# Another order of the rows within each expert's 64-row tile, in a two-layer MLA, sliding-window and MoE step

## The reference

```
def hier_moe(x, ...):                      # 32 experts in 4 groups of 8, FF = 512
    g_p, g_idx = top_k(softmax(xt @ w_group + b_group), 1)
    e_top, e_idx = top_k((xt @ w_expert + b_expert) of that group, 2)
    gate = g_p * softmax(e_top)
    ...
    hid = silu(xb @ w_gate[e]) * (xb @ w_up[e])     # xb: the rows of expert e
    yb = hid @ w_down[e]
    y = sum over a token's two experts of gate * its row of yb
```

## Time and profile before

| | us |
|---|---|
| median of three runs | 1774.24 |
| the runs | 1773.89, 1774.24, 1779.27 |
| the profiled execution | 1780.06 |
| its span, first to last instruction | 1778.4 |
| PE busy | 1677.9 |
| DVE busy | 651.8 |
| ACT busy | 381.2 |
| POOL busy | 216.2 |

### The profile page before, as it was taken

The page is one execution under the profiler, slowest core; times in us unless marked ns, Lnnn a source line. Parts: engine busy times, 40 slices in busy tenths (PEclk is TensorE's granted clock), DMA queues, the critical chain, the costliest instruction groups (busy, mean ns, idle before and its releaser), DMA issues.

```text
span 1778.4 us, 27879 instructions
## 1 busy us (share of the span) xinstructions
PE 1677.9 (94%) x9782; PEld 822.3 (46%) x9783; DVE 651.8 (37%) x1593; ACT 381.2 (21%) x878; POOL 216.2 (12%) x313
## 2 busy tenths in 40 slices
PE   7899899889899999999998899999899999999995
PEld 5466665545544444444443445455344444444432
DVE  2333588742322222222221656764322222222214
ACT  2233445531111111111110234342111111111112
POOL 1232025400010000101011201000001010101000
PEclk9899999989999999999999899999899999999997
DMA  6154139875489999999998800135799999999994
GB/s 188 50 157 115 28 124 309 282 273 224 157 343 404 422 416 423 410 422 413 421 411 335 306 1 1 28 136 227 274 386 418 420 420 419 417 414 417 410 378 159
DMA packets 84883, 513.81 MB, mean 289 GB/s; under 512 B 20821, under 2 KB 43302, under 8 KB 58586
## 3 DMA queue, kind: packets, MB, share of 16 engines
q1 hardware_dynamic: 66378, 463.45, 64.8%
q0 software_dynamic: 18416, 49.16, 8.5%
HBM read 499.65 MB, written 26.52 MB: 296 GB/s over the span
## 4 chain that ended last, share of the span: by engine, by line
PE 80%; DMA 7%; DVE 6%; issue 2%; ACT 2%; DVEq 1%; SPq 1%; ACTq 1%; POOLq 0%
PE ps L2080 72%; PE ps L2085 8%; DMA mem<-in_moe_w_up 4%; DMA mem<-in_cache_mla 2%; ACT mem L801 1%; DVE mem L1373 1%; SPq L482 1%; DVE mem L1859 0%; ACTq L982 0%; DMA mem<-in_mla_w_a 0%; DMA mem<-moe_rows_back 0%; DVE mem L1830 0%; DVEq L1381 0%; DVE mem L1822 0%; DMA mem<-in_mla_wq_b 0%
## 5 line engine op out<-in xcount | busy, mean ns | idle before, releaser
L2080 PE MATMUL ps<-mem 128*64 128x512 f32 (+14 forms) x8398 | 1513.9, 477 | 55.3 <-ACT mem L801 14.8
L2080 PEld LDWEIGHTS ps<-mem 128*64 128x64 f32 (+5 forms) x8398 | 659.0, 146 | 825.3 <-issue 741.4
L801 ACT ACTIVATE mem<-ps 128x512 f32<-128x512 f32 (+7 forms) x358 | 193.5, 546 | 552.6 <-PE ps L2080 392.0
L2085 PE MATMUL ps<-mem 64*128 64x64 f32 (+3 forms) x1384 | 202.6, 281 | 37.7 <-issue 7.6
L2085 PEld LDWEIGHTS ps<-mem 64*128 64x128 f32 (+3 forms) x1384 | 168.3, 182 | 122.2 <-issue 97.4
L1698 DVE TENSOR_TENSOR mem<-mem,ps 64x512 f32<-64x512 f32 x64 | 44.1, 690 | 408.0 <-ACT mem L1051 407.8
L736 POOL DMA_INDIRECT moe_rows_back<-mem x64 | 57.3, 896 | 818.6 <-DVE mem L1716 810.3
L1051 ACT ACTIVATE mem<-ps 64x512 f32<-64x512 f32 x64 | 37.7, 589 | 519.2 <-PE ps L2080 519.2
L1373 DVE STREAM_TRANSPOSE mem<-mem 128x2560 f32<-128x2560 f32 x32 | 89.2, 2824 | 17.5 <-DMA mem<-in_cache_mla 17.2
L1716 DVE COPY mem<-ps 64x512 f32<-64x512 f32 x64 | 44.4, 693 | 133.3 <-PE ps L2080 133.2
L686 POOL DMA_DIRECT2D mem<-in_cache_mla x96 | 51.5, 537 | 75.5 <-PE ps L2080 68.2
(11 more groups left out here) (238 smaller groups left out, 534.2 us busy)
## 6 DMA issues: line engine op xcount, KB each, us to landing
mem<-in_moe_w_gate SPq DMA_DIRECT2D x64, 2048.0 KB
mem<-in_moe_w_up SPq DMA_DIRECT2D x64, 2048.0 KB
mem<-in_moe_w_down SPq DMA_DIRECT2D x64, 2048.0 KB
mem<-in_cache_mla POOLq DMA_DIRECT2D x160, 160.0 KB, 3.6
mem<-in_cache_mla SPq DMA_DIRECT2D x96, 160.0 KB, 4.5
mem<-moe_rows_back SPq DMA_DIRECT2D x8, 1024.0 KB, 8.9
mem<-in_mla_wkv_b SPq DMA_DIRECT2D x8, 512.0 KB, 6.5
mem<-in_mla_wo SPq DMA_DIRECT2D x1, 4096.0 KB, 14.2
```

Source lines behind the costliest of these rows:

```text
L801: return act.activation(out, in_, ACT.Copy)
L2080: return pe.matmul(out, lhsT, rhs, start=start, stop=stop)
L2085: return pe.transpose(out, in_, ident[at:at + n, at:at + n])
```

## The change

A table `spread` with two rows of 64 numbers is added and filled once by DVE. `spread[0]` holds, at row c * 32 + 2 * e + a of the tile, the rank c * 32 + 16 * a + e (c and a are 0 or 1, e is 0 to 15); `spread[1]` the same with 15 - e for e. `mark` compares with `spread[b]`, where b is 0 for even experts and 1 for odd ones, instead of `slots`; the loop over extra blocks compares with `spread[0]`. So of an expert with n rows, the first 16 stand one in each pair of rows of the tile's lower half, the next 16 fill these pairs, and the rest do the same in the upper half; in odd experts the pairs are taken from the other end. The tensor `mem` grows by 80 words and `keep` by 128, so that what lies behind moves.

```diff
-        WORDS = 53120
+        WORDS = 53200
...
         consts = mem[:, TILES * D:keep.at]
+        spread = [keep.take(BLK) for _ in range(2)]
...
             latent_T(PT)
+            by_rank = slots.rearrange("p (c a e) -> p c a e", c=2, a=2)
+            by_row = [s.rearrange("p (c e a) -> p c a e", c=2, a=2) for s in spread]
+            v.tensor_copy(by_row[0], by_rank)
+            for e in range(BLK // 4):
+                v.tensor_copy(by_row[1][:, :, :, BLK // 4 - 1 - e:BLK // 4 - e], by_rank[:, :, :, e:e + 1])
             v.tensor_copy(pick.rearrange("p j (i r) -> p j i r", i=4),
...
                 def mark(q, b):
 
                     v.tensor_tensor(onehot[b], rankm[:, :, cols(q, 1)].broadcast_to([P, TILES, BLK]),
-                                    slots.unsqueeze(1).broadcast_to([P, TILES, BLK]), ALU.is_equal
+                                    spread[b].unsqueeze(1).broadcast_to([P, TILES, BLK]), ALU.is_equal
                                     ).then_inc(sig["onehot_ready"], 1)
...
                         v.tensor_tensor(onehot[0], shift.unsqueeze(2).broadcast_to([P, TILES, BLK]),
-                                        slots.unsqueeze(1).broadcast_to([P, TILES, BLK]), ALU.is_equal
+                                        spread[0].unsqueeze(1).broadcast_to([P, TILES, BLK]), ALU.is_equal
                                         ).then_inc(sig["more_marks"], 1)
```

## The result

The changed kernel takes 1767.05 us (median of 19 runs, 1761.32 to 1775.18). The kernel before, run beside it and before it, takes 1778.57 us (median of 19, 1772.46 to 1783.2). The ratio on record is 0.995 with a 95% interval of 0.9939 to 0.9961, that is 6.9 to 10.8 us less; the two medians by themselves are 11.5 us apart. A later repeat gave 0.995 again (0.9931 to 0.9969). The profiled execution went from 1780.06 to 1769.54 us.

What follows compares the result with a forecast made beforehand. PE sets the pace until each MoE stage's last experts, where weights come late behind one or two overloaded DMA engines. 7.0 (layer 0) + 6.5 (layer 1) = 13.5 us off gives 1762.0 us, own range 1757 to 1767, wide 1757 to 1771.

Steps and rivals of the forecast that it cites:

- The map and the rows: Both MoE stages: DMA engine j serves rows 2j, 2j+1, 32+2j, 33+2j; busiest falls from 149 to 112 and 156 to 116.
- blocks of four: Rival map for the MoE tiles: engine j serves rows 4j to 4j+3, so no change, 1772 us; chance 8%.
- handicap: Slower rival: engine 15 slow of itself, hidden under its few rows; at 8 us 1778, at most 1789; chance 4%.
- the costs put at nothing: DVE's 17 new copies, at most 3.9 us, covered by its idle time; other table and shifted addresses: zero.
- The slow clock: PE's slower clock behind late weights at the stages' ends: 1.70 us in layer 0, 2.80 in layer 1, to go.
- I take 5.2, the smaller: Layer 0's end: busiest DMA engine finishes 5.2 us earlier, the estimate from tails, not 5.9 from its rows; layer 1 5.3.
- layer 1's 6.5 us: Layer 1's end: both PE waits for weights and the slow clock go, 0.48 + 3.25 + 2.80 us.
- all engines late together: Rival: evened queues still behind PE, waits of 0.2 to 1 us stay; gain 9 to 10, 1765 to 1769; chance 12%.
- a margin of 0.8 us: Layer 0's end: last weights there at 942.6, PE asks for them at 943.35, so waits of 4.5 us go.
- so I take 966.5: Joint between the layers: layer 0's last scatter lands at 966.5, between 963.0 and 968.8, 7.0 us before 973.5.
- Layer 0 in all: Layer 0's end and the joint to layer 1: 7.0 us less, 4.5 of it the waits.
- The base: Whole kernel: profiled execution lay 5.8 us above the runs' median; 1762.0 leaned to 1760.7 rather than 1766.5.

Runs made afterwards that it cites:

- e4: Changed kernel with ranks 4j to 4j+3 all put on rows 2j, 2j+1, 32+2j, 33+2j in all experts: 1790.22 us, 1.0089 of the kernel before.
- e3: Changed kernel with even experts in rank order and odd ones in that order with pairs taken from 15 down: 1774.39 us, 0.9996 of the kernel before.
- e1: Changed kernel with both tables filled in rank order, keeping tables, copies and addresses: 1777.94 us, 1.0016 of the kernel before.
- e7: Changed kernel with ranks 4j to 4j+3 on one engine, odd experts from the other end: 1790.66 us, 1.0079 of the kernel before.
- e8: Changed kernel with only the even experts' ranks 4j to 4j+3 put on one engine: 1773.96 us, 0.999 of the kernel before.
- e6: Changed kernel with the second part of layer 1's wqkv issued behind SP's first load of rows_back: 1770.63 us, 0.9954 of the kernel before.
- e5: Changed kernel with the gathers' index bound at 0, so odd experts' gathers carry no rows: 1755.72 us, 0.9894 of the kernel before.
- e2: Changed kernel with ranks dealt over the pairs from pair 0 up in all experts, no reversal: 1767.94 us, 0.9967 of the kernel before.

## Why the prediction was right or wrong

**The map and the rows** were right. Rank order in the same code gives the old time, the increments of layer 1's last scatter show the rows where the map has them (2, 1 and 13 engines with none, one and two rows before, 9, 1 and 6 with none, three and four in e4), blocks of four are refuted by e4's 1.0089 too and rows j, j + 16 by e3, and the lag fell from 6.6 to 1.5 us in layer 0 and from 6.8 to 1.4 in layer 1: by 5.1 and 5.4 us, where 5.2 and 5.3 had been forecast. By the map engine 15 has nearly the most rows after the change (111 of 112 and 116 of 116), and the lag of 1.5 and 1.4 us is no longer than the rows make it (1.5 and 1.8): no handicap shows here.

**Right: the costs put at nothing.** e1 bounds copies, other table and addresses together at -0.02% to +0.34%; DVE shows 4.95 us of idle behind the copies where I had said some 4.

**The slow clock.** The sums use 1.70 and 2.80 us for it. They are 12.22 and 13.32 us less 10.52 for the same 48 records, and what the runs show of its cause is the granted clock beside them: before, 0.60 in 932.93 to 937.00 and 0.50 in 1726.80 to 1729.00, behind waits of 1.60 and 3.25 us; after, 0.50 in 1717.66 to 1720.00, behind the wait of 1.34 us. Behind those of 1.16 us before and 0.54 after the block took 10.52 us.

**Wrong: the size of the step "I take 5.2, the smaller".** The last up weights came only 3.5 us earlier in layer 0 (from 947.81 to 945.91, though PE came to this stretch 1.63 us later) and 3.8 in layer 1 (from 1726.80 to 1717.66, of which 5.35 us are PE's own earlier arrival, 1667.38 to 1662.03). I had let the busiest engine fall to a mean that stands still. It does not stand still: the mean landing of the last down weights came 1.4 us later in layer 0 (49.9 to 51.3) and 1.5 in layer 1 (50.7 to 52.2), and 5.1 - 1.4 = 3.7 and 5.4 - 1.5 = 3.9 are near the 3.5 and 3.8 found.

Why the mean came later is less sure. The order of the odd experts' rows can move the rate, as e7 and e8 show (409 and 404 GB/s against 416 and 412), and in layer 0 the two kernels in rank order have the earliest means (49.9 and 50.2) and the highest rate (417) of those that gather rows; the others with a mean in the table have 50.8 to 52.1 and 415 or 416. But in layer 1 rank order in the new code has a mean of 51.8, 1.1 us later than the same order before: two executions can differ by most of the 1.5 us. Dealt one way has 50.2 there, the earliest. That the new order itself costs the rate something is likely in layer 0 and open in layer 1. Nor is it clear why the pairs reversed have so late a mean (53.6) in layer 1: their rates in the table, 415 and 412, are those of the repeated changed kernel, which keeps its gain.

So 0.54 and 1.34 us of wait stayed, one with a slow clock of 1.68 us behind it. Of layer 1's 6.5 us only 6.53 - 1.34 - 1.68 = 3.5 went; 1.70 more came from the slow stretch at 1680 that went too. I had put it at nothing because I had not seen it; it hung on the same late weights, and the sum would have been 1.70 us larger, and further off, with it. This is the rival "all engines late together", to which I gave 12%: its 9 to 10 us and 1765 to 1769 are what happened (10.5 us in the profile, 8.9 by the ratio, 1767.05). It is also the sign of being wrong that I had named, a tail that shrinks while waits stay. Its condition was there to be read: a margin of 0.8 us in layer 0 under a sum whose one term, 5.2, had no allowance for the rate. For layer 1 I had a margin of 1.5 us, and 1.34 us of wait stayed all the same.

**Wrong: the step "so I take 966.5".** Scatter landed at 971.2, and 968.1 was forecast (966.5 and the 1.63 us by which this execution was late). I reasoned that most engines are idle two to three microseconds after the issue. That was true of the uneven queue, where 14 of the 16 engines had landed their rows 4.81 us after the issue; in the even one most work until 968 to 970 (share 1.03 in 967 to 968, 0.55 in 969 to 970), the scatter's rows stand behind their loads, and the first engine lands its rows 5.89 us after the issue. The worst end that I gave, the new end of the busiest engine, was nearly the right one: 968.8 + 1.63 = 970.4. Layer 0 in all gave 4.6 us and not 7.0. e6 and e5 show the cause: with wqkv's bytes moved or the queues shorter the scatter takes 3.6 us.

**The base.** 1762.0 leaned on a median of 1774.24 us of three runs. Nineteen gave 1778.57. That is 4.3 us of the 5.05 by which the time was missed. The gain itself was forecast as 12.2 us from the median; it was 11.5 between the medians and 8.9 by the ratio. So the direction and the mechanism were right and the gain was forecast too large, by about 3 us in the profiled execution. 1767.05 lies inside the wide range (1757 to 1771) and just outside my own (1757 to 1767).

## What to carry to other kernels

When a transfer carries few rows, count bytes per DMA engine, not per transfer. Here the busiest engine had, by the map, 46 and 51 rows over the mean of 103 and 104.5, and the last down weights, split over all 16, landed 6.6 and 6.8 us behind the mean of their increments; with 9 and 12 rows over it was 1.5 and 1.4 us. Evening it out helped only down to the length of the queue as a whole: 0.54 and 1.34 us of wait stayed, which went when the gathers carried no rows. A small DMA that had slipped in behind idle engines then stood behind busy ones: the first increments of layer 0's last scatter came 2.45 us after its issue before and 5.89 us after. Before taking a queue's mean as fixed, compare its GB/s at full share with and without the odd transfers in it, here 416 and 413 against 427 and 425.

## What the runs showed of the hardware

- In a GpSimd-issued indirect DMA of 64 rows of 4096 B, one engine serves rows 2j, 2j+1, 32+2j and 33+2j, for j from 0 to 15 (that j is also the engine's number is my naming; the traces name no engine). This rests on the increments of layer 1's last scatter (13 engines with two of 27 rows in rank order at 2.33 to 2.54 us, 6 with four in e4 at 2.94 to 3.12, 6 with four in e7 at 3.07 to 3.23), which show it for j from 0 to 6 and 9 to 15, on the steps of the tail, on the order of e1, e2, the change and e4 (1.0016, 0.9967, 0.995, 1.0089) and on the lags of the table.
- A row that is out of bounds stands in the trace as a packet of 4 B that takes 9 ns, a row of 4096 B as one of 159 ns, both in the median of the kernel before; in layer 1's last scatter of that kernel, which lands in 2.54 us, the 27 rows took 199 to 335 ns each.
- With the same 48 records PE takes 10.52 us at a granted clock of 1.00, 12.22 us where it was 0.60 in the first 4.07 us, and 13.32 us where it was 0.50 in the first 2.20 us and 0.57 in the next 4.
- A gather from DRAM lowers the rate of the weight transfers beside it: 348 to 352 GB/s for 4 us against 414 when it carries no rows, all with the DMA share full, and 21.8 to 21.9 GB/s against 26.6 in the weights' own packets of one engine. With four rows on each engine used it was 309 in one kernel, with the stage's rate at 409 and 404; in another (four to one) the stage kept 416 and 412. Even experts' scatters with four rows on an engine leave it at 416 and 412. Why a gather does this, at its source or in its destination, stays open.
- The rows of the 32 gathers are a third of all rows, and taking them away was worth 12.4 us, more than the whole change. By their bytes they are 34 x 0.159 = 5.4 us of each queue in a layer; the last down weights landed 15.8 and 16.0 us earlier on the mean.
